# The token transform split into a cosine and a sine half, and the chunk inverse in blocks of 64 on opposite quarters of TensorE

## The reference, cut to what matters

```python
def step(state, inp):                      # rwkv7_time_mix, 512 tokens, 4 heads of 64
    r_t, w_t, k_t, v_t, kk_t, a_t = inp
    sa = jnp.einsum('bhij,bhj->bhi', state, -kk_t)
    state = (state * w_t[:, :, None, :] + sa[..., None] * (kk_t * a_t)[:, :, None, :]
             + v_t[..., None] * k_t[:, :, None, :])
    return state, jnp.einsum('bhij,bhj->bhi', state, r_t)
...
def fourier_mix(p):                        # each layer: 512 tokens; layer 0 also 256 context tokens
    b, n, _ = p.shape
    g = p.reshape(b, n, N_FOURIER, HEAD_DIM).astype(jnp.float32)
    f = jnp.fft.fft2(g, axes=(1, 3), norm='ortho').real
    return f.reshape(b, n, GROUP_W).astype(p.dtype)
```

## Time and profile before

| | us |
|---|---|
| median of three runs | 2271.06 (2270.22 to 2274.23) |
| the profiled execution | 2269.8 |
| its span, first to last instruction | 2268.0 |
| TensorE busy in the span | 2160.7 (95%) |
| VectorE, ScalarE, GpSimd busy | 1219.3, 738.0, 54.5 |
| mean granted TensorE clock | 0.971 |

### The profile page before, as it was taken

How to read it: one execution, slowest core, us unless ns; L and a number is a source line. 1 busy time by engine, 2 the same in 40 slices (tenths; PEclk the granted TensorE clock), 3 DMA queues, 4 the chain that set the end, 5 groups by cost and what they waited for, 6 DMA issues and landing times.

```text
span 2268.0 us, 29476 instructions
## 1 busy us (share of the span) xinstructions
PE 2160.7 (95%) x11330; PEld 1711.8 (75%) x11330; DVE 1219.3 (54%) x1923; ACT 738.0 (33%) x1154; POOL 54.5 (2%) x97
## 2 busy tenths in 40 slices
PE   6999899999999989989999999999999999999999
PEld 5678785447777767878888888887777676888887
DVE  4654332345544566466666664336447556666644
ACT  4612111354324454241111123224245443222232
POOL 0002020000001000000000000000010000000000
PEclk9999999899999989999999999999999899999999
DMA  5441214772112200111111112111122012222322
GB/s 185 158 158 41 72 48 155 269 262 84 56 56 57 98 1 1 56 43 60 65 65 65 57 64 67 56 63 63 59 65 107 1 38 75 94 100 92 102 93 84
DMA packets 51392, 189.04 MB, mean 83 GB/s; under 512 B 5904, under 2 KB 5904, under 8 KB 50656
## 3 DMA queue, kind: packets, MB, share of 16 engines
q1 hardware_dynamic: 46752, 168.32, 21.9%
q0 software_dynamic: 3168, 16.54, 2.1%
q10 hardware_dynamic: 1376, 2.85, 0.3%
HBM read 184.53 MB, written 3.15 MB: 83 GB/s over the span
## 4 chain that ended last, share of the span: by engine, by line
PE 86%; DVE 8%; ACT 3%; issue 2%; DMA 1%; ACTq 0%; DVEq 0%; SPq 0%; POOLq 0%
PE psum L228 22%; PE psum L230 21%; PE psum L229 21%; PE psum L649 3%; PE psum L683 3%; PE psum L673 2%; PE psum L1761 2%; PE psum L2142 1%; PE psum L1315 1%; PE psum L661 1%; PE psum L1326 1%; PE psum L1323 1%; DVE h_low L386 1%; PE psum L1304 1%; PE psum L1871 1%
## 5 line engine op out<-in xcount | busy, mean ns | idle before, releaser
L228 PE MATMUL psum<-h_high,unit_high 128*128 128x512 f32 (+1 forms) x1792 | 659.6, 368 | 14.2 <-DVE h_low L386 6.1
L230 PE MATMUL psum<-h_high,unit_low 128*128 128x512 f32 (+1 forms) x1792 | 645.7, 360 | 0.0
L229 PE MATMUL psum<-h_low,unit_high 128*128 128x512 f32 (+1 forms) x1792 | 644.2, 359 | 0.0
L228 PEld LDWEIGHTS psum<-h_high,unit_high 128*128 128x128 f32 x1792 | 340.8, 190 | 90.1 <-issue 18.9
L420 ACT CAST unit_high<-ring 128x1024 fp32r<-128x1024 f32 x194 | 203.0, 1047 | 612.4 <-PE psum L230 611.8
L230 PEld LDWEIGHTS psum<-h_high,unit_low 128*128 128x128 f32 x1792 | 340.0, 190 | 54.4
L428 DVE TENSOR_TENSOR unit_low<-ring,unit_high 128x1024 fp32r<-128x1024 f32 x194 | 237.0, 1222 | 265.5 <-ACT unit_high L420 265.5
L229 PEld LDWEIGHTS psum<-h_low,unit_high 128*128 128x128 f32 x1792 | 340.6, 190 | 49.2 <-issue 0.7
L2309 DVE TENSOR_SCALAR conv_out<-psum,parameters 128x512 f32<-128x512 f32 (+1 forms) x132 | 91.2, 719 | 176.7 <-PE psum L230 176.7
L2314 DVE SCALAR_TENSOR_TENSOR conv_out<-psum,parameters,conv_out 128x511 f32<-128x511 f32 (+1 forms) x264 | 166.4, 658 | 22.2 <-DVE conv_out L2309 1.5
L750 ACT ACTIVATE probs<-psum,neg_max 128x768 f32<-128x768 f32 (+4 forms) x136 | 98.7, 728 | 180.9 <-DVE neg_max L711 168.5
(11 more groups left out here) (375 smaller groups left out, 2670.8 us busy)
## 6 DMA issues: line engine op xcount, KB each, us to landing
ring<-in_w_units SPq DMA_DIRECT2D x317, 512.0 KB, 3.3
dft<-in_dft POOLq DMA_DIRECT2D x2, 2048.0 KB, 8.2
bias<-in_na_bias POOLq DMA_DIRECT2D x2, 1536.0 KB, 12.3
xT<-in_x ACTq DMA_DIRECT2D x4, 512.0 KB, 6.5
xT<-in_x POOLq DMA_DIRECT2D x1, 2048.0 KB, 11.4
constants_first<-in_constants_first POOLq DMA_DIRECT2D x1, 1361.0 KB, 9.3
xT<-in_ctx POOLq DMA_DIRECT2D x1, 1024.0 KB, 15.8
rope<-in_rope POOLq DMA_DIRECT2D x2, 512.0 KB, 3.4
```

The costliest lines, as they stand in the source:

```text
L228: pe.matmul(out, lh, rh, start=first, stop=False, skip_group_check=True)
L229: pe.matmul(out, lh, rl, start=False, stop=False, skip_group_check=True)
L230: return pe.matmul(out, ll, rh, start=False, stop=last, skip_group_check=True)
```

## The change

**Chunk inverse.** The doubling runs in the two diagonal blocks of 64 up to level 5, and level 6 joins them. `a_mat`, `t_mat` and `t_t` keep only the diagonal blocks: rows 0 to 63 hold the first block's 64 columns, rows 64 to 127 the second's. `t_two` holds both forms of the inverse, 512 columns in one bank and one tile, so that one VectorE addition takes the place of two. Each M and T product is now two of 64x64, the first on rows and columns 0 to 63 of the array, the second on 64 to 127, in turn. At level 6 only the lower left block is needed, one 64x64 product per head each for M and T, and VectorE copies it into `t_t`; at level 5 VectorE waits for its own addition and copies both diagonal blocks into `t_t`. GpSimd has one mask operation of 256 columns per level and buffer, and none at level 6. ScalarE's copy of M has 256 columns instead of 512.

**Token transform.** The table `dft` holds cosines of 0 to 256 and sines of 1 to 255, 512 columns in all where there were 1024. The cosine part (257 columns) and the sine part (255) go into the two halves of the bank. ScalarE copies the sine part to `odd`; VectorE writes columns 0 and 256, the sum and, in reverse order, the difference, and only then frees the bank. The scale moves to the features copy.

`constants_first` is 512 columns narrower. The diff, cut to its core:

```diff
@@ -1307,24 +1311,33 @@
-            pe.wait_ge(x_ready[b].sem, x_ready[b].base + n + 1)
+            if lev < STEPS:
+                pe.wait_ge(x_ready[b].sem, x_ready[b].base + g * (STEPS - 1) + lev)
...
-                mm = pe.matmul(K.ps[M_BANK[b]][:, hd * P:hd * P + P], x_mat[b][:, e, i], t_t[b][:, e, i],
-                               start=True, stop=True)
+                to = K.ps[M_BANK[b]][:, hd * HD:hd * HD + HD]
+                if lev == STEPS:
+                    mm = pe.matmul(to[halves[0]], a_mat[b][halves[1], 1, e, i], t_two[b][halves[1], 0, e, i],
+                                   start=True, stop=True)
+                else:
+                    for rows in halves:
+                        mm = pe.matmul(to[rows], x_mat[b][rows, e, i], t_two[b][rows, 0, e, i], start=True, stop=True)
...
-                pe.matmul(K.ps[T_BANK[b]][:, hd * P:hd * P + P], t_mat[b][:, e, i], m_mat[b][:, e, i],
-                          start=True, stop=True)
-            for hd, (e, i) in enumerate(heads):
-                mm = pe.matmul(K.ps[T_BANK[b] + 1][:, hd * P:hd * P + P], m_mat[b][:, e, i], t_mat[b][:, e, i],
-                               start=True, stop=True)
+                for rows in halves[:1 + (lev < STEPS)]:
+                    mm = pe.matmul(K.ps[T_BANK[b]][rows, hd * HD:hd * HD + HD], t_two[b][rows, 1, e, i],
+                                   m_mat[b][rows, 0, e, i], start=True, stop=True)
+            if lev < STEPS:
+                for hd, (e, i) in enumerate(heads):
+                    for rows in halves:
+                        mm = pe.matmul(K.ps[T_BANK[b]][rows, 2 * P + hd * HD:2 * P + hd * HD + HD],
+                                       m_mat[b][rows, 0, e, i], t_two[b][rows, 1, e, i], start=True, stop=True)
...
@@ -1394,16 +1407,16 @@
-            for lev in range(1, LEVELS):
+            for lev in range(1, STEPS):
...
-                    mask = const(K, "level")[:, lev * P:lev * P + P]
-                    for e in range(2):
-                        ins = pool.tensor_tensor(x_mat[b][:, e], a_mat[b][:, e], wide(mask), ALU.mult)
-                    x_ready[b].up(ins)
+                    mask = const(K, "level")[:, lev * HD:lev * HD + HD]
+                    x_ready[b].up(pool.tensor_tensor(x_mat[b].rearrange("p e i t -> p (e i) t"),
+                                                     a_mat[b][:, 0].rearrange("p e i t -> p (e i) t"), four(mask),
+                                                     ALU.mult))
...
@@ -1513,19 +1526,26 @@
             if g:
-                dve.wait_ge(x_ready[b].sem, x_ready[b].base + g * STEPS)
+                dve.wait_ge(x_ready[b].sem, x_ready[b].base + g * (STEPS - 1))
             prod = lambda n, e: K.ps[3 * e + n // 2][:, (n % 2) * 2 * P:(n % 2) * 2 * P + 2 * P] \
                 .rearrange("p (i t) -> p i t", i=2)
+            both = lambda ap: ap.rearrange("p e i t -> p (e i) t")
             for e in range(2):
-                ins = dve.tensor_copy(a_mat[b][:, e], prod(0, e))
+                for rows in halves:
+                    ins = dve.tensor_copy(a_mat[b][rows, 0, e], prod(0, e)[rows, :, rows])
             taken.up(ins)
             for e in range(2):
-                dve.tensor_tensor(t_mat[b][:, e], prod(0, e), wide(const(K, "level")[:, 0:P]), ALU.mult)
-                ins = dve.tensor_tensor(t_t[b][:, e], prod(1, e), wide(const(K, "level0_t")), ALU.mult)
+                dve.tensor_copy(a_mat[b][halves[1], 1, e], prod(0, e)[halves[1], :, halves[0]])
+                for rows in halves:
+                    mask = const(K, "level0_t")[rows].unsqueeze(1).to_broadcast([HD, 2, HD])
+                    ins = dve.tensor_tensor(t_two[b][rows, 0, e], prod(1, e)[rows, :, rows], mask, ALU.mult)
+            dve.wait_ge(taken.sem, taken.base + c + 1)
+            ins = dve.tensor_tensor(both(t_two[b][:, 1]), both(a_mat[b][:, 0]), four(const(K, "level")[:, 0:HD]), ALU.mult)
             link(dve, K.dve_step, ins)
-            for e in range(2):
-                dve.tensor_tensor(t_mat[b][:, e], t_mat[b][:, e], wide(const(K, "ident")), ALU.add)
-                dve.tensor_tensor(t_t[b][:, e], t_t[b][:, e], wide(const(K, "ident")), ALU.add)
+            for which in range(2):
+                dve.tensor_tensor(both(t_two[b][:, which]), both(t_two[b][:, which]), four(const(K, "ident_half")), ALU.add)
+            if g == 0:
+                dve.memset(t_t[b][halves[1], :, :, 0:HD], 0.0)
             for e in range(2):
...
@@ -1535,8 +1555,16 @@
             dve.wait_ge(t_up[b].sem, t_up[b].base + g * STEPS + lev)
-            dve.tensor_tensor(flat(t_t[b]), flat(t_t[b]), K.ps[T_BANK[b]][:, :], ALU.add)
-            t_out[b].up(dve.tensor_tensor(flat(t_mat[b]), flat(t_mat[b]), K.ps[T_BANK[b] + 1][:, :], ALU.add))
+            if lev == STEPS:
+                new = K.ps[T_BANK[b]][halves[0], 0:2 * P].rearrange("p (e i t) -> p e i t", e=2, i=2)
+                t_out[b].up(dve.tensor_copy(t_t[b][halves[0], :, :, HD:P], new))
+                return
+            room = t_two[b].rearrange("p w e i t -> p (w e i t)")
+            t_out[b].up(dve.tensor_tensor(room, room, K.ps[T_BANK[b]][:, :], ALU.add))
+            if lev == STEPS - 1:
+                dve.wait_ge(t_out[b].sem, t_out[b].n)
+                for rows in halves:
+                    dve.tensor_copy(t_t[b][rows, :, :, rows], t_two[b][rows, 0])
...
@@ -1724,7 +1752,8 @@
-                    m_out[b].up(act.copy(flat(m_mat[b]), K.ps[M_BANK[b]][:, :]))
+                    rows = slice(0, HD if lev == STEPS else P)
+                    m_out[b].up(act.copy(flat(m_mat[b][:, 0])[rows], K.ps[M_BANK[b]][rows, 0:2 * P]))
...
@@ -2136,11 +2165,11 @@
-            count = last - first
-            for e in range(count):
-                for q in range(2):
-                    mm = pe.matmul(bank[:, 0:w], z[:, e, q * P:q * P + P], dft[:, q, e, 0:S:S // w],
-                                   start=(e == 0 and q == 0), stop=(e == count - 1 and q == 1))
+            count, middle, step = last - first, w // 2, S // w
+            cosines, sines = slice(0, S // 2 + 1, step), slice(S // 2 + step, S, step)
+            for q, (c, to) in enumerate(((cosines, bank[:, 0:middle + 1]), (sines, bank[:, middle + 1:w]))):
+                for e in range(count):
+                    mm = pe.matmul(to, z[:, e, q * P:q * P + P], dft[:, e, c], start=(e == 0), stop=(e == count - 1))
...
@@ -2180,11 +2209,17 @@
         first, last, w = parts[part]
+        dve.wait_ge(bank_up.sem, bank_up.base + t + 1)
         if kind == "tokens":
-            return
-        dve.wait_ge(bank_up.sem, bank_up.base + t + 1)
-        if kind == "features":
-            bank_free.up(dve.tensor_copy(z[:, tile:tile + 2, :], bank[:, :].rearrange("p (t f) -> p t f", f=2 * P)))
+            to, middle = p[:, FO + n, first * P:first * P + w], w // 2
+            dve.wait_ge(z_ready.sem, z_ready.base + 1 + n + 2 * part)
+            even, sine_part = bank[:, 1:middle], odd[:, 0:middle - 1]
+            dve.tensor_copy(to[:, 0:middle + 1:middle], bank[:, 0:middle + 1:middle])
+            dve.tensor_tensor(to[:, 1:middle], even, sine_part, ALU.add)
+            bank_free.up(dve.tensor_tensor(to[:, w - 1:middle:-1], even, sine_part, ALU.subtract))
+        elif kind == "features":
+            bank_free.up(dve.tensor_scalar(z[:, tile:tile + 2, :], bank[:, :].rearrange("p (t f) -> p t f", f=2 * P),
+                                           float((w * HD) ** -0.5), None, ALU.mult))
         elif kind == "gate":
...
@@ -2209,11 +2244,9 @@
-            _, n, part, _ = uses[t]
-            first, last, w = parts[part]
+            w = parts[uses[t][2]][2]
...
-            bank_free.up(act.activation(p[:, FO + n, first * P:first * P + w], bank[:, 0:w], ACT.Identity,
-                                        scale=float((w * HD) ** -0.5)))
+            z_ready.up(act.copy(odd[:, 0:w // 2 - 1], bank[:, w // 2 + 1:w]))
...
@@ -2825,8 +2859,10 @@
-    put("level", level.reshape(P, -1))
-    put("level0_t", level[:, 0].T)
+    half = lambda m: np.concatenate([m[:HD, :HD], m[HD:, HD:]])
+    put("level", np.concatenate([half(level[:, n]) for n in range(LEVELS - 1)], axis=1))
+    put("level0_t", half(level[:, 0].T))
+    put("ident_half", half(np.eye(P)))
...
@@ -2838,8 +2874,8 @@
-    both = np.stack([np.cos(angle), np.sin(angle)])
-    return np.ascontiguousarray(both.reshape(2, NT, P, S).transpose(2, 0, 1, 3)).astype(np.float32)
+    both = np.concatenate([np.cos(angle)[:, 0:S // 2 + 1], np.sin(angle)[:, 1:S // 2]], axis=1)
+    return np.ascontiguousarray(both.reshape(NT, P, S).transpose(1, 0, 2)).astype(np.float32)
...
```

(23 more changed lines are left out.)

## The result

The changed kernel took 2234.53 us (median of 4 runs, 2234.19 to 2235.80) where the kernel before, run beside it, took 2270.64 (4 runs, 2264.02 to 2274.23). The ratio is 0.984, with a 95% interval of 0.9818 to 0.9864: 36.1 us less, and 2232 had been forecast. The profiled execution took 2234.19 us around a span of 2232.4.

What follows compares the result with a forecast made beforehand. The prediction took TensorE to bound the kernel. Saving 26.6 us in the chunk inverse and 12.0 in the token transform, 38.6 in all, from the median 2271.06 gave 2232 us, with a range of 2223 to 2250.

Steps and rivals of the forecast that it cites:

- What bounds it: Whole kernel: TensorE carries 86% of the chain that ended last, so work taken off it is gained.
- The level, 4.97: Chunk inverse, levels 1 to 5: M 0.92, T 1.85 and two slots of 1.10 make 4.97 us, where 6.87 stood.
- the slot: Chunk inverse: three filling products plus the changes between full-size and small tiles take 1.10 us, twice a level.
- (a): Chunk inverse: opposite quarters don't overlap, a level takes 7.75 us, total 2260; chance 0.12.
- The circle: Chunk inverse: M, ScalarE copy, T, VectorE addition, M keeps up with 4.97 us, about 1 us cover, 0.2 at level 5.
- `take_products`, 5.5: Ahead of the inverse: VectorE's ten half-width pieces at 0.2 us, nine full ones and a memset still make about 5.5 us.
- Tokens, 12.0: Token transform: shorter products save 6.6 us in layer 0 and 5.6 in layer 1, less 0.2 for the scaled copy.
- The sum: Whole kernel: 26.6 us from the inverse plus 12.0 from the token transform, 38.6 saved.
- (b): Chunk inverse: TensorE isn't fed every 0.029 us; at 0.058 a level takes 5.9 us, total 2242; chance 0.12.
- (c): Inverse levels: granted clock falls to 1.2 GHz, a level takes 8.9 us, total 2278, slower; chance 0.05.
- (d): Token transform: brings nothing since VectorE's queue eats the gain, total 2244; chance 0.06.

Runs made afterwards that it cites:

- the first one-slot kernel: Changed kernel with one piece of six fill products a level behind T instead of two of three, and ScalarE's copy-out one level later: 2234.56 us.
- after: The changed kernel's first profiled execution, the trace compared first with the kernel before: 2234.19 us.
- after again: The changed kernel, unchanged, run again on one chip beside the kernel before: 2229.99 us, ratio 0.984.
- after third: The changed kernel, unchanged, run once more beside the kernel before and the kernel with three further edits: 2228.88 us, ratio 0.9844.
- the inverse alone: Kernel before with only the chunk inverse in blocks of 64, token transform as before: 2236.46 us, ratio 0.9869.
- the tokens alone: Kernel before with only the token transform changed, chunk inverse as before: 2256.66 us, ratio 0.9964.

## Why the prediction held

It forecast 2232 and its range was 2223 to 2250; measured were 2234.5, 2230.0 and 2228.9 in three sets of runs. Point by point:

- **What bounds it.** TensorE was the bound and stayed so: 28.27 busy of 28.28 us in the group.
- **The level, 4.97.** Measured 4.88. M and T as summed (0.93 and 1.85); the slot was mis-sized, 1.05 (180.98 - 179.93) for the 1.10 that I took from the rows behind the levels. The group is 28.24 for 28.8 and so 13.85 is saved for 13.3. That the opposite quarters overlap, taken from two indirect rows, was right: rival (a) had 7.75 a level.
- **The circle.** The cover of about 1 us is there (182.86 to 183.88). At level 5 buffer 1's addition ends 5.19 after the level's start and its next product starts at 5.40: the 0.2 to spare of the forecast. How little spare there was the first one-slot kernel shows: there a 1.23 us operation that waited for ScalarE and stood ahead of the additions was enough to lose 1.0 a group.
- **`take_products`, 5.5.** This step failed. Ten pieces of half the width were put at 0.2 each, by halving 0.34. The operations are also half the partitions, and the four of L1535 take 1.19 (153.52 to 154.64, 0.28 each). Other rows of after separate the two: one operation of 64x256 (L1560) takes 0.42 as one of 128x256 does (0.41, L1552), and 128x128 (L1590) takes 0.28 as 64x128 does (0.29, L1538). So halving the partitions saves nothing, and halving the columns a third and not half. It is 6.5, and costs 0.6 per group at the full clock; the forecast had nothing.
- **Tokens, 12.0.** Measured 6.55 + 5.68 = 12.2. From the token product to the two features products 7.37 and 11.87 were forecast and 7.40 and 11.77 measured. Use by use, 1.66, 3.1 and twice 0.9 were forecast in layer 0 and 1.76, 3.38, 0.88 and 0.53 measured, in layer 1 2.2 and 3.4 against 2.29 and 3.39 (after again). The order of ScalarE's queue had been read right, with the square ahead of the copy. It was taken as given, though, and was worth 2.3 us more.
- **What comes back later.** The sum had nothing for it, and I had followed each queue through the changed stages and not behind them. The modulation products wait some 1 to 2.7 us more for weights in the traces of the changed kernel, part of it in exchange for clock. But the stretch that holds them was shorter in after again, after third and the inverse alone (504.4 to 505.3) than before (506.7 and 512.0), so no run shows that this costs time.
- **The sum.** 27.7 - 1.2 + 12.2 is 38.7 at the full clock, against 38.6 forecast and 36.1, 38.5 and 38.7 measured. Two errors of opposite sign (the slot and level 6 +1.1, the products taken out -1.2) cancelled; that is luck and no merit of the method. So is the closeness of whole times: stretches that the change doesn't touch differed by 7 us and more between executions.
- **The rivals.** (a) fell with 4.88, and literally: two row halves of TensorE wrote one bank at the same time, in different partitions, 32 instructions in 0.93 us. (b) fell as well: a load and a product every 0.029 us held for 1.85 us; with it falls, for this kernel, the 62 ns per product that the prediction cited from the Trainium skill ("TensorE: Matmul & The Clock Gate", Back-to-back issue gap). (c) didn't come: 1.00 in the levels. (d) fell by the tokens alone.

## What to carry to other kernels

In a block-diagonal product of 128x128 that is bound by its loads, two 64x64 products on opposite quarters of TensorE took half the time here (2.78 us a level where 48 loads at 0.11 are 5.3). The two quarters must take turns, one instruction or at most four at a time; eight at a time cost 1.0 us of a level. Each change between such tiles and full-size ones cost 0.36 us to and fro, so put filling work into few, long pieces. When an engine is made faster, list what stands ahead in each queue that hands it something, including operations on ScalarE or GpSimd that have nothing to do with it, and go on past the changed stage to the next transfer. Where executions differ by more than an edit is worth, compare the starts of a stage in two traces at the same clock: here they agree to 0.02 us, while medians of whole runs move by several. And before a difference in an untouched stretch is explained, look at that stretch in a second trace of either kernel.

## What was not expected of the hardware

- TensorE doesn't start products in program order when they lie on different quarters: it took the first of a free quarter with three of the busy one ahead, 0.2875 us after the busy quarter's first in place of 0.464.
- At granted clock 1.00 the same instructions of one program ran at 197.1, 199.7 or 200.0 us in different executions (after, after third, after again), and each of 14 traced executions of eleven programs had one of these three. What sets it stays open; neither the program nor the chip does so alone.
- In a row VectorE needs 0.28 to 0.30 us for each operation of 64x128 elements out of PSUM where one of 128x256 needs 0.34. A single one of 64x256 takes as long as one of 128x256 (0.42 and 0.41): splitting along the partitions doubled the cost.
